# RMS norm of the softmax attention's output in a hybrid decoder step: the sum and the spread over partitions by tokens, root and reciprocal on six columns

## The reference

```python
o_s = swa_fn(qs, ks, vs, sinks)
o_s = rmsnorm(o_s, swa_g)        # over the 512 features of a token
x = x + jnp.concatenate([o_g, o_s], axis=-1) @ w_out
def rmsnorm(x, g):
    return x * lax.rsqrt(jnp.mean(x * x, axis=-1, keepdims=True) + EPS) * g
```

## Time and profile before

| what | value |
|---|---|
| time, median of 3 runs | 2044.79 us (2044.76 to 2045.3) |
| the profiled execution's own time | 2051.94 us |
| its span, first to last instruction | 2050.1 us |
| mean granted TensorE clock in it | 0.975 |
| busy: TensorE, VectorE, ScalarE, GpSimd | 1984.1, 1367.3, 1103.4, 1092.0 us |

### The profile page before, as it was taken

One profiled execution on the slowest core, in us unless ns is written; L12 is line 12 of the kernel. 1 busy time (PEld: TensorE's weight loads), 2 busy tenths in 40 slices (PEclk: granted clock), 3 DMA queues, 4 the chain that ended last, 5 costly groups with the idle time before them and its releaser, 6 DMA issues.

```text
span 2050.1 us, 40879 instructions
## 1 busy us (share of the span) xinstructions
PE 1984.1 (97%) x15562; PEld 1944.9 (95%) x15562; DVE 1367.3 (67%) x2490; ACT 1103.4 (54%) x2178; POOL 1092.0 (53%) x807
## 2 busy tenths in 40 slices
PE   5999999999999999999999999999999999999997
PEld 5999999998889999999999999999898999999997
DVE  7876677586345776577678757766753458756874
ACT  4664566546234565466656646663631356645662
POOL 3665566632114566566756656665221156655664
PEclk9999999999879999999999999999997899999998
DMA  3233233321212233223323333323120122332331
GB/s 133 78 108 105 88 98 101 129 83 53 86 34 81 70 104 108 89 99 99 98 73 104 98 99 101 103 94 133 63 96 32 55 88 78 103 104 89 98 103 65
DMA packets 92114, 185.65 MB, mean 91 GB/s; under 512 B 12880, under 2 KB 22768, under 8 KB 91376
## 3 DMA queue, kind: packets, MB, share of 16 engines
q1 hardware_dynamic: 84096, 170.04, 25.2%
q10 hardware_dynamic: 7824, 13.01, 1.8%
HBM read 178.09 MB, written 6.95 MB: 90 GB/s over the span
## 4 chain that ended last, share of the span: by engine, by line
PE 93%; DVE 4%; issue 2%; ACT 1%; DMA 0%; POOLq 0%; POOL 0%; DVEq 0%; ACTq 0%
PE ps L798 54%; PE ps L758 23%; PE ps L807 7%; PE ps L1027 1%; PE ps L1140 1%; PE ps L1016 1%; PE ps L1134 1%; PE ps L1179 1%; PE ps L1193 1%; PE ps L786 1%; PE ps L1207 1%; PE ps L999 0%; DVE h_end L1665 0%; PE ps L1168 0%; PE ps L778 0%
## 5 line engine op out<-in xcount | busy, mean ns | idle before, releaser
L798 PE MATMUL ps<-rhs,w_hi 128*128 128x272 f32 x4256 | 806.1, 288 | 12.4 <-issue 12.4
L798 PEld LDWEIGHTS ps<-rhs,w_hi 128*128 128x128 f32 x4256 | 670.0, 188 | 13.9 <-issue 13.9
L798 PE MATMUL ps<-rhs,w_lo 128*128 128x272 f32 x2128 | 614.0, 289 | 0.0
L646 POOL TENSOR_TENSOR w_lo<-w_raw,w_hi 128x512 fp32r<-128x512 f32 x272 | 354.6, 1310 | 272.4 <-ACT w_hi L1295 272.4
L640 POOL TENSOR_TENSOR w_lo<-w_raw,w_hi 128x1024 fp32r<-128x1024 f32 x80 | 190.7, 2386 | 447.5 <-ACT w_hi L1239 432.3
L798 PEld LDWEIGHTS ps<-rhs,w_lo 128*128 128x128 f32 x2128 | 402.3, 189 | 0.0
L798 PE MATMUL ps<-act_c,w_hi 128*128 128x272 f32 x1792 | 355.9, 289 | 5.9 <-ACT d_tmp L1400 3.0
L798 PEld LDWEIGHTS ps<-act_c,w_hi 128*128 128x128 f32 x1792 | 287.9, 188 | 7.7 <-ACT d_tmp L1400 3.9
L646 POOL TENSOR_TENSOR w_lo<-s_tmp,w_hi 128x512 fp32r<-128x512 f32 x216 | 280.9, 1312 | 25.2 <-ACT w_hi L1295 25.0
L758 PE MATMUL ps<-h_mid,w_hi 128*128 128x272 f32 x1600 | 284.7, 297 | 0.0
L798 PE MATMUL ps<-act_c,w_lo 128*128 128x272 f32 x896 | 258.3, 288 | 0.0
(11 more groups left out here) (290 smaller groups left out, 3321.2 us busy)
## 6 DMA issues: line engine op xcount, KB each, us to landing
w_raw<-stream SPq DMA_DIRECT2D x380, 256.0 KB, 2.9
w_raw<-stream SPq DMA_DIRECT2D x80, 512.0 KB, 3.3
g_buf<-stream SPq DMA_DIRECT2D x52, 256.0 KB, 2.8
pl_raw<-stream SPq DMA_DIRECT2D x64, 192.0 KB, 2.8
x<-xT ACTq DMA_DIRECT2D x8, 272.0 KB, 6.2
y_d<-x SPq DMA_DIRECT2D x8, 272.0 KB, 2.1
s<-s_d ACTq DMA_DIRECT2D x2, 1024.0 KB, 4.9
s_s_d<-s ACTq DMA_DIRECT2D x2, 1024.0 KB, 3.8
```

The source lines that it names most:

```text
L646: pool.tensor_tensor(operand(w_lo, j, half), source(op, s, half), operand(w_hi, j, half).bitcast(F32), ALU.subtract).then_inc(pool_low, 1)
L798: ins = pe.matmul(bank(s, at), w[:, k * P:(k + 1) * P], moving[:, k, side, r, :], start=fresh and k == 0 and w is hi and side == 0, stop=k ...
```

## The change

The job `squares` stays in the list as a name for its PSUM pair 0, but TensorE runs nothing for it, and it isn't counted in `in_used` any more (`evacuated`). `s_add` and `s_norm` are gone. In slot 18, between `kv` 3 and `gs_kv` 0, TensorE runs `s_sum`: for each of the six pieces and each of the four squared tiles a fp32 product with that piece as weights and one column of ones, accumulated over the four tiles into one column of pair 0. ScalarE takes the root of the six columns into `sst`. Behind `gs_kv` 1, VectorE takes the reciprocal (`s_recip`) and waits for the spread. TensorE does the spread in the middle of the tile `rG2`, after 24 of its 48 products, into pair 0. `smix` reads the factor from PSUM there, 0 and 1 in slot 18, 2 at the head of slot 19 ahead of `att` 2, 3 at its end. `out0`, which writes pair 0 next, waits for all four.

```diff
-            18: [("att", 1), ("o", 0), ("kv", 2), ("kv", 3), ("gs_kv", 0), ("gs_kv", 1), ("s_add", 0)],
-            19: [("att", 2), ("o", 1), ("kv", 4), ("kv", 5), ("gs_kv", 2), ("gs_kv", 3)],
-            20: [("s_norm", 0), ("smix", 0), ("smix", 1)],
-            21: [("att", 3), ("smix", 2), ("o", 2), ("kv", 6), ("kv", 7), ("smix", 3)] +
+            18: [("att", 1), ("o", 0), ("kv", 2), ("kv", 3), ("s_sum", 0), ("gs_kv", 0), ("gs_kv", 1),
+                 ("s_recip", 0), ("smix", 0), ("smix", 1)],
+            19: [("smix", 2), ("att", 2), ("o", 1), ("kv", 4), ("kv", 5), ("gs_kv", 2), ("gs_kv", 3), ("smix", 3)],
+            21: [("att", 3), ("o", 2), ("kv", 6), ("kv", 7)] +
...
+            def square_spread():
+
+                pe.wait_ge(m["s_recip"], 2)
+                pe.wait_ge(m["in_used"], JOBS.index("squares") - 1)
+                for c, (at, w) in enumerate(PIECES):
+                    ins = pe.matmul(squares()[:, at // TH, at % TH:at % TH + w], sst[0:w, c:c + 1].to_broadcast([w, P]),
+                                    ident[0:w, 0:w], start=True, stop=True)
+                ins.then_inc(m["s_spread"], 1)
...
                         if name == "squares":
-                            pe.wait_ge(m["s_added"], 1)
-                            ins = square_sum(dst, sq_tile(0))
-                            ins.then_inc(m["ssum_done"], 1)
                             continue
                         if name[:3] == "out":
+                            if name == "out0":
+                                pe.wait_ge(m["mix_made"], 4)
...
+                    elif step == "s_sum":
+                        pe.wait_ge(m["ssq"], 4)
+                        pe.wait_ge(m["in_used"], JOBS.index("squares") - 1)
+                        for c, (at, w) in enumerate(PIECES):
+                            for j in range(4):
+                                ins = pe.matmul(squares()[0:w, 0, c:c + 1], sq_tile(j)[:, at:at + w], ones[:, 0:1],
+                                                start=j == 0, stop=j == 3)
+                        ins.then_inc(m["ssum_done"], 1)
...
-                    elif step == "s_norm":
+                    elif step == "s_sum":
                         act.wait_ge(m["ssum_done"], 1)
-                        act.activation(halves(sq_tile(0)), pair(job_pair(JOBS.index("squares"))), ACT.Sqrt,
-                                       bias=eps[:, :], scale=1.0 / (4 * P)).then_inc(m["s_root"], 1)
+                        w = PIECES[-1][1]
+                        act.activation(sst[:, 0:4], squares()[:, 0, 0:4], ACT.Sqrt, bias=eps[:, :],
+                                       scale=1.0 / (4 * P)).then_inc(m["s_root"], 1)
+                        act.activation(sst[0:w, 4:6], squares()[0:w, 0, 4:6], ACT.Sqrt, bias=eps[0:w, :],
+                                       scale=1.0 / (4 * P)).then_inc(m["s_root"], 1)
...
-                    elif step == "s_add":
-                        dve.wait_ge(m["ssq"], 4)
-                        for j in range(1, 3):
-                            link(dve.tensor_tensor(sq_tile(0), sq_tile(0), sq_tile(j), ALU.add))
-                        dve.tensor_tensor(sq_tile(0), sq_tile(0), sq_tile(3), ALU.add).then_inc(m["s_added"], 1)
-                    elif step == "s_norm":
-                        dve.wait_ge(m["s_root"], 1)
-                        dve.reciprocal(sq_tile(0), sq_tile(0)).then_inc(m["in_used"], 1)
-                        dve.wait_ge(m["in_used"], JOBS.index("squares") + 1)
+                    elif step == "s_recip":
+                        dve.wait_ge(m["s_root"], 2)
+                        w = PIECES[-1][1]
+                        dve.reciprocal(sst[:, 0:4], sst[:, 0:4]).then_inc(m["s_recip"], 1)
+                        dve.reciprocal(sst[0:w, 4:6], sst[0:w, 4:6]).then_inc(m["s_recip"], 1)
+                        dve.wait_ge(m["s_spread"], 1)
                     elif step == "smix":
-                        dve.scalar_tensor_tensor(out=qS[:, i, :], in0=qS[:, i, :],
-                                                 scalar=lp[:, SG + i:SG + i + 1], in1=sq_tile(0),
+                        dve.scalar_tensor_tensor(out=halves(qS[:, i, :]), in0=halves(qS[:, i, :]),
+                                                 scalar=lp[:, SG + i:SG + i + 1], in1=squares(),
```

More of the change, by code:

```diff
@@ L109, in in_chunk, with evacuated @@
     raise KeyError(name)
+def evacuated(i):
+    return i - (i > JOBS.index("squares"))
 def job_pair(i):
@@ L267, in trunk @@
         nrt = sb("nrt", [P, len(PIECES)])
+        sst = sb("sst", [P, len(PIECES)])
         assert plan["at"] <= nc.sbuf_usable_end, plan["at"]
@@ L406, in sq_tile, with squares @@
             return (g_buf, sq_buf)[j // 2][:, j % 2, :]
+        def squares():
+            return pair(job_pair(JOBS.index("squares")))
         def go_out():
@@ L494, in trunk @@
                    "ga_out", "go_done", "go_out", "klm_made", "gkv_done", "gkv_used", "r_silu",
-                   "gsq", "gss_done", "g_root", "g_recip", "gbc_done", "ssq", "s_added", "ssum_done", "s_root", "q_paired",
+                   "gsq", "gss_done", "g_root", "g_recip", "gbc_done", "ssq", "ssum_done", "s_root", "s_recip", "s_spread", "q_paired",
                    "mix_made", "mix_high", "mix_ready", "kb_made"]
@@ L761, in product, with model_tile @@
                 return ins
-            def model_tile(dst, chunk, slot, h, stage=None, middle=None):
+            def model_tile(dst, chunk, slot, h, stage=None, middle=None, inside=None):
                 pe.wait_ge(lo_ready, chunk + 1)
@@ L770, in model_tile @@
                         norm_spread(middle)
+                    if k == KT // 2 and inside is not None:
+                        inside()
                     ins = product(dst, slot, k * P, h[:, 0, k, :], h[:, 1, k, :], k == 0, k == KT - 1)
@@ L944, in mixer @@
                         if i >= 3:
-                            pe.wait_ge(m["in_used"], i - 1)
+                            pe.wait_ge(m["in_used"], evacuated(i - 1))
                         dst = pair(job_pair(i))
                         if name == "squares":
-                            pe.wait_ge(m["s_added"], 1)
-                            ins = square_sum(dst, sq_tile(0))
-                            ins.then_inc(m["ssum_done"], 1)
                             continue
                         if name[:3] == "out":
+                            if name == "out0":
+                                pe.wait_ge(m["mix_made"], 4)
                             output_half(ch, 0, int(name[3]), dst)
@@ L974, in mixer @@
                             ins = model_tile(dst, ch + c, (PL_MIX + c) % RING, h_mid,
-                                             stage if i == 0 else None, stage if i == 1 else None)
+                                             stage if i == 0 else None, stage if i == 1 else None,
+                                             square_spread if name == "rG2" else None)
                         ins.then_inc(chunk_done, 1)
@@ L1214, in mixer @@
                     if n == 2:
-                        pe.wait_ge(m["in_used"], len(JOBS))
+                        pe.wait_ge(m["in_used"], evacuated(len(JOBS)))
                     if n >= 4:
@@ L1568, in mixer @@
                     elif step == "silu":
-                        act.wait_ge(m["in_used"], JOBS.index(f"rG{i}") + 1)
+                        act.wait_ge(m["in_used"], evacuated(JOBS.index(f"rG{i}") + 1))
                         act.activation(rG[:, i, :], rG[:, i, :], ACT.Silu).then_inc(m["r_silu"], 1)
@@ L2275, in mixer @@
                             low_part(7, a_buf[:, i % 2, :])
-                dve.wait_ge(m["in_used"], len(JOBS))
+                dve.wait_ge(m["in_used"], evacuated(len(JOBS)))
                 def evacuate(n):
```

## The result

| | before | changed |
|---|---|---|
| median of 5 runs, us | 2044.79 (2043.92 to 2045.3) | 2056.39 (2051.84 to 2059.27) |
| ratio | | 1.0051 [1.0034, 1.0068] |
| profiled execution, us (span; mean granted clock) | 2051.94 (2050.1; 0.975) | 2051.84 (2050.0; 0.978) |

The account below looks back on a forecast made before the run. TensorE, busy 97% of the span, bounds the kernel. Per layer -1.60 -1.67 +5.3 +1.6 +0.2 +0.8 = +4.6, two layers +9.2 us: profiled 2051.94 to 2061.1, less 7.15 for the median, 2054.0 us; range 2046.5 to 2061.

Parts of the forecast that it names:

- What bounds the kernel: Whole program: TensorE, busy 97% of the span; VectorE or ScalarE time counts only where TensorE stands still for it.
- `squares` removed: Mixer norm on TensorE: two 272-column fp32 products go, -1.60 us per layer; additions, root and reciprocal priced at nothing.
- the wait for `klm`: End of slot 18, before L1179: TensorE's wait is covered by `s_sum`, -1.67 us per layer.
- `s_sum`, 5.3 per layer: In place of the wait before `gs_kv` 0: 48 records added, +5.3 us per layer, bounds 4.2 and 8.2.
- Spread, 1.6: Middle of `rG2`: 12 records added on TensorE, +1.6 us per layer, up to 3.0 at the lower clock; no stall.
- The mask, 0.2: Slot 19 on VectorE: moved `smix` 2 and `low_part` make the mask of `att` 2 late, +0.2 us per layer (0 to 0.4).
- Rival 3: Mask of `att` 2 late, so `kv` 4 and followers up to 2 us late per layer: 2057.6 us, chance 0.08.
- The clock afterwards, 0.8 per layer: `gs_kv` steps and `rG2` behind `s_sum` run longer at the lower clock: +0.8 us per layer on average.
- Rival 1: Clock holds through `s_sum` because the gap is filled: +0.4 us per layer, 2045.6 us, no change, chance 0.16.
- Rival 2: Rival 1, and `out0` meets the full clock in both layers: another -2.5 us each, 2040.6 us, chance 0.08.
- Assumed: Profiled execution to median: the changed kernel's median lies 7.15 us below its profiled execution, as before.

Follow-up runs that it names:

- mask first: Changed kernel with `smix` 2 behind the mask of `att` 2 in slot 19 instead of ahead of it: 2055.14 us, ratio 1.0042 to before.
- the thin one: Kernel before with 12 unused one-column fp32 records put in TensorE's wait for `klm`: 2044.03 us, ratio 1.0004.
- dense filling: Kernel before with two unused 272-column fp32 products (four records) put in TensorE's wait for `klm`: 2042.56 us, ratio 0.9987.
- late `smix`: early squares with `smix` back in its old places, 0 and 1 in slot 20, 2 and 3 in slot 21: 2044.82 us, ratio 0.9997.
- early squares: Kernel before with its own norm moved earlier: additions ending slot 17, two 272-column products before `gs_kv` 0, `smix` in slots 18 and 19: 2036.30 us, again 2036.69.

## Why the prediction was right

**What bounds the kernel**: right. VectorE's 10.5 us bought nothing; an added sum alone cost as much as the change.

**`squares` removed, 1.60, and the wait for `klm`, 1.67 per layer**: both gone. Counted from `att` 1, `rG2` ends 7.1 us later in layer 0 (21.91 against 14.85), where 6 to 7 were expected, and 5.4 in layer 1. A later wait of 0.6 us before `gs_kv` 3 is not new, it is the rest of the 2.2 in the earlier trace rows.

**`s_sum`, 5.3 per layer**: 6.36 and 5.30 us, 5.83 on average, so 1.1 us too little over both layers. The record lengths were right (0.11 us wide at the upper level, 0.21 at the lower where 0.20 was taken). What failed is the sentence "I let the clock fall at the same times". In layer 0 the fall was put 2.5 us behind the start of the sum (557.2, with L1106 ending near 554.7) and came 1.2 behind it; in layer 1 it was put 1.9 behind it and came 2.35. The first made the term 1.3 too small, the second 0.3 too large. For the Trainium skill's figure (TensorE: Matmul & The Clock Gate, LDWEIGHTS: columns divided by 1.2 GHz), the two distances decide: 0.45 us for four wide records at the upper level, 0.85 at the lower. The figure fits the first alone. The 1.9 us that the prediction puts on the difference leave the 16 narrow records out; with its own 0.045 us for each of them the estimate is 1.2.

**Spread, 1.6**: its records take 1.53 us in both layers. What it does to the whole is less sure: 6.4 us alone in the kernel before, not resolved in the changed one.

**The mask, 0.2**: 0 and 0.24 us of wait, and the order of `smix` and mask makes no measurable difference. The subtraction stretched to 2.79 us, as priced from 2.72. Rival 3 fell. Its counterargument, that the product now reads PSUM, holds for the product (0.77 us beside GpSimd in mask first), not for the subtraction behind it.

**The clock afterwards, 0.8 per layer**: this is the term that was undersized, by more than `s_sum`. The forecast as a whole puts some 3 us into the clock (1.06 per layer in `s_sum` over its 4.24, 0.8 after it, less about 0.4 for `squares`, which lose their slow stretch); the runs show +7.9 on one chip and, for the changed kernel's own five runs against 44 for the kernel before, about +5. The full-clock part grew by 4 to 5 us, where the forecast's other terms make 6. The sum came out near because one error offset part of the other. From `att` 1 to the GLA norm's sums, the stretches in which the whole 9.2 us were forecast, both profiles of the changed kernel show +8.5 us against before (60.65 and 59.34 us in the two layers of the first, 59.36 and 60.63 in those of the second). With a single profile of before it stays open where the rest of the 11.6 to 13.1 us lies. The 5.3 us at the lower level in layer 1 of before, from which 0.6 was worked out, stand in no row ahead; its trace has the clock at 1.00 again from 1567.6, which agrees.

**Rival 1** (the clock holds in a filled gap) is wrong for the work that fills it: in `s_sum` and in the sum added to before TensorE had no idle time and fell to 0.50 all the same. The two fillings leave the same half microsecond of wait; behind the thin one the clock fell, behind two 272-column products it held. The prediction had the sign of the first half in its row at 608 to 610, and did not ask what wider products in the gap would do. The Trainium skill (same page, Why this matters for your kernels) warns of long idle gaps between bursts of matmuls. Here the clock fell and stayed low without any gap, with 5.00 us busy of 5.00 at 0.50. **Rival 2** saw one thing rightly: `out0` met the full clock in layer 0 of the profiled run. It did not decide the median.

**Assumed**: that the changed kernel's profiled run lies 7 us above its median like that of before. It lay 4.5 below. The difference of two medians was forecast, so the assumption did no harm; reading the two profiles' spans against each other would have given "no change".

**Open**: why the spread alone costs 6.4 us in the kernel before, twice its records, why the dense filling gives back more than it keeps, and why the late `smix` costs the whole gain of early squares. All three are in the clock part; no run set the moment at which the clock falls by itself, so it is argued and not shown that later dense groups merely meet other levels.

## What to carry to other kernels

Relieving an engine that nobody waits for is worth nothing, and paying for it with one-column fp32 products on the bounding engine costs 5.3 to 6.4 us for 48 records, most of them at the lower clock, where, once VectorE has added the tiles, two 272-column products do it in 1.2 to 1.6. If a wait of TensorE is to be filled, fill it with wide products that are needed anyway, and read the granted clock behind it; then look again at what follows on the other engines, since a chain that was covered may end last once TensorE arrives earlier. Compare medians, and split each run by its clock before two profiles are compared.

## What was not expected of the hardware

One kernel's runs spread over 13 us (2051.51 to 2064.49) with no change of its work: time multiplied by the mean clock stays within 2004.6 to 2007.3 for these six. The kernel before spreads less, with rare runs some 12 us up (2056.27 and 2057.63 among 17).

In the same gap of 1.7 us, four records of 272 columns and twelve of one column last equally long (1.18 and 1.23 us), and behind them the same `rG2` takes 6.20 or 8.36 us.

Beside a GpSimd subtraction a VectorE product with an operand in PSUM stayed at 0.77 us (mask first), while the same product on SBUF operands took 2.72 (before) and a subtraction of the same size 2.04 to 2.79. Without GpSimd beside them, these take 0.7 to 0.8.
